# Eight of twenty modulation chunks moved from the first mixer into the first projection

## The reference

```python
for i in range(DEPTH):                                    # DEPTH = 2
    mod_x = jnp.split(jax.nn.silu(c) @ w_mod[i] + b_mod[i], 6, axis=-1)
    mod_c = jnp.split(jax.nn.silu(c_ctx) @ w_mod[i] + b_mod[i], 6, axis=-1)
    hx = modulate(rms_norm(x, norm1[i]), mod_x[0], mod_x[1])
    hc = modulate(rms_norm(ctx, norm1[i]), mod_c[0], mod_c[1])
    ...
# even mixer: proj = h @ w_in; qkv = silu(dwconv_centred(qkv, w)); q, k l2-normalised;
# gated DeltaNet over the chunks, both directions; gate, norm, @ w_out
```

## Time and profile before

| | before |
|---|---|
| three runs, us | 2581.56, 2587.11, 2586.36 |
| median, us | 2586.36 |
| the profiled execution, us | 2585.57 |
| its span, us | 2583.7 |
| mean granted clock of PE, share of full | 0.837 |
| PE / DVE / ACT / POOL busy, share of the span | 69% / 64% / 37% / 38% |
| DMA, mean over the span | 362 GB/s |

### The profile page before, as it was taken

How to read it: one execution, slowest core, us unless ns; L and a number is a source line. 1 busy time by engine, 2 the same in 40 slices (tenths; PEclk the granted TensorE clock), 3 DMA queues, 4 the chain that set the end, 5 groups by cost and what they waited for, 6 DMA issues and landing times.

```text
span 2583.7 us, 35131 instructions
## 1 busy us (share of the span) xinstructions
PE 1779.7 (69%) x13040; PEld 842.2 (33%) x13040; DVE 1664.7 (64%) x3921; ACT 956.5 (37%) x2624; POOL 979.3 (38%) x895
## 2 busy tenths in 40 slices
PE   5998889797867695557655565557957765565554
PEld 4877666445532251112211121113533311111111
DVE  2545657769996665677766776654466666766665
ACT  2411147444342332335533353333333433333333
POOL 2013123344443333444444444441023444445442
PEclk8999989898997897768887787778988877767777
DMA  8279769999899999999999999995168999999997
GB/s 310 98 252 324 279 254 370 390 387 393 335 366 417 415 398 409 421 397 419 419 419 421 394 421 419 421 421 212 66 266 356 421 421 421 392 412 421 421 421 292
DMA packets 181899, 936.20 MB, mean 362 GB/s; under 512 B 18128, under 2 KB 35408, under 8 KB 82400
## 3 DMA queue, kind: packets, MB, share of 16 engines
q0 software_dynamic: 114912, 808.16, 76.3%
q1 hardware_dynamic: 66816, 125.79, 13.4%
HBM read 932.74 MB, written 1.15 MB: 361 GB/s over the span
## 4 chain that ended last, share of the span: by engine, by line
DMA 40%; PE 32%; DVE 10%; issue 6%; ACT 6%; POOL 4%; another core or an unknown queue 0%; SPq 0%; DVEq 0%; POOLq 0%; ACTq 0%
DMA arena<-in_experts,expert_cur 38%; PE ps L1170 12%; PE ps L1950 11%; DVE arena L2031 5%; POOL arena L1863 4%; ACT diag L1883 2%; PE ps L1182 2%; DMA wring<-in_ev_w_in 2%; PE ps L1717 2%; PE ps L1195 2%; ACT coef L1879 1%; PE ps L1395 1%; DMA arena<-in_w_mod 1%; ACT acts L1878 1%; PE ps L1218 1%
## 5 line engine op out<-in xcount | busy, mean ns | idle before, releaser
L1950 PE MATMUL ps<-arena,diag 64*64 64x512 f32 x6144 | 1007.8, 784 | 664.9 <-ACT diag L1883 635.0
L1863 POOL DMA_INDIRECT arena<-in_experts,expert_cur x768 | 910.8, 1186 | 1333.8 <-PE ps L1950 1013.9
L2031 DVE CUSTOM_DVE_ANT_0 arena<-arena 128x1024 f32<-128x1024 f32 x768 | 943.3, 1229 | 613.9 <-DMA arena<-in_experts,expert_cur 605.6
L1950 PEld LDWEIGHTS ps<-arena,diag 64*64 64x64 f32 x6144 | 244.9, 161 | 1340.6 <-ACT diag L1883 961.7
L1878 ACT ACTIVATE acts<-dots 128x2 f32<-128x2 f32 x384 | 78.2, 204 | 1068.2 <-DVE dots L2031 1067.7
L1883 ACT ACTIVATE diag<-consts,coef 128x128 f32<-128x128 f32 x768 | 266.1, 393 | 12.5
L1879 ACT ACTIVATE coef<-acts,gate_cur 128x1 f32<-128x1 f32 x768 | 184.8, 288 | 12.6
L1170 PE MATMUL ps<-wring 128*128 128x256 f32 (+2 forms) x568 | 148.9, 414 | 29.6 <-DVE arena L815 15.3
L1170 PEld LDWEIGHTS ps<-wring 128*128 128x128 f32 x568 | 100.7, 195 | 94.7 <-issue 72.6
L1170 PE MATMUL ps<-arena,wring 128*128 128x256 f32 (+1 forms) x576 | 114.3, 357 | 6.4 <-issue 5.6
L1737 POOL DMA_DIRECT2D mods<-straight x48 | 26.7, 559 | 212.6 <-DVEq L1732 212.6
(11 more groups left out here) (331 smaller groups left out, 1813.0 us busy)
## 6 DMA issues: line engine op xcount, KB each, us to landing
wring<-in_w_mod SPq DMA_DIRECT2D x18, 2048.0 KB, 9.7
wring<-in_ev_w_in SPq DMA_DIRECT2D x14, 1024.0 KB, 24.6
arena<-in_w_mod SPq DMA_DIRECT2D x6, 2048.0 KB, 10.3
wring<-in_ev_w_in SPq DMA_DIRECT2D x6, 2048.0 KB, 10.4
arena<-in_experts,expert_cur POOLq DMA_INDIRECT x768, 11.8
wring<-in_p_w_q SPq DMA_DIRECT2D x5, 2048.0 KB, 27.4
wring<-in_ev_w_out SPq DMA_DIRECT2D x3, 2048.0 KB, 24.9
wring<-in_od_w_out SPq DMA_DIRECT2D x2, 2048.0 KB, 7.6
```

The costliest lines, as they stand in the source:

```text
L1863: nc.gpsimd.indirect_dma_start(ring[:, k % RING, :], None, table, bass.IndirectOffsetOnAxis(ap=expert_cur[:, par, k:k + 1], axis=0),).then ...
L1950: last = nc.tensor.matmul(ps[rows_of(o), sum_bank(i, c), :], diag[rows_of(i), slot, rows_of(i)], ring[rows_of(i), slot, D + 512 * c:D + 51 ...
L2031: ins = nc.vector.tensor_tensor_reduce(out=ring[:, slot, 0:D], in0=ring[:, slot, 0:D], in1=place, scale=1.0, scalar=0.0, op0=ALU.mult, op1 ...
```

## The change

Mod 4 to mod 11 leave the mixer and are multiplied between the stages of the first projection. The mixer keeps mod 12 to mod 23, still one a stage from stage 8 on, so now in stages 8 to 19. The list of first loads is written out by hand with its slots: the loads of the seven projection blocks and of the eight chunks alternate, and the chunks use slots 2 and 3 only. The sixteen loads behind them get hand-written slots too. The bodies of `mod_pe`, `mod_dve` and all sums are the same.

```diff
 def beside(main, rest, part=lambda n: None):
-    n = N_COLUMNS
+    n = N_COLUMNS + len(MODS_EARLY)
...
+def with_mods(main, part):
+
+
+    for i, _ in enumerate(main):
+        if i in MODS_EARLY:
+            part(N_COLUMNS + MODS_EARLY.index(i))
...
+MODS_EARLY = (2, 4, 5, 6, 8, 9, 10, 12)
 W_IN_ORDER = (3, 4, 5, 1, 2, 0, 6)
+FIRST_LOADS = [(3, 0), (4, 1), ("mod", 2), ("mod", 3), ("mod", 2), (5, 0), ("mod", 3), ("mod", 2), (1, 1), ("mod", 3),
+               ("mod", 2), (2, 0), ("mod", 3), (0, 2), (6, 3)]
...
-    loads = [(n, last, i % 4) for i, (n, last) in enumerate(loads)]
...
+    others = mods[n:]
+    others += [(("w_out0", 0, c), ("out0", 1, c)) for c in range(2)]
+    others += [(("w_q0", 0, c), ("q0", 0, 4 * c + 3)) for c in range(2)]
+    loads += [(name, last, (1, 0, 2, 3, 1, 3, 0, 2, 3, 1, 0, 2, 3, 0, 1, 2)[i]) for i, (name, last) in enumerate(others)]
...
-                whole(qkv_dve(dve, 0))
+                with_mods(qkv_dve(dve, 0), lambda n: mod_dve(dve, n))
...
-                whole(qkv_pe(pe, 0))
+                with_mods(qkv_pe(pe, 0), lambda n: mod_pe(pe, n))
```

More of the change, by code:

```diff
@@ L295, in weight_loads @@
     mods = [(("mod", i, c), ("mod", i, c)) for i, c in MODS]
-    loads = mods[:N_COLUMNS] + w_in_loads() + mods[N_COLUMNS:]
-    loads += [(("w_out0", 0, c), ("out0", 1, c)) for c in range(2)]
-    loads += [(("w_q0", 0, c), ("q0", 0, 4 * c + 3)) for c in range(2)]
-    loads = [(n, last, i % 4) for i, (n, last) in enumerate(loads)]
+    last_of, n = dict(w_in_loads()), N_COLUMNS
+    loads = [(*mod, i) for i, mod in enumerate(mods[:N_COLUMNS])]
+    for what, slot in FIRST_LOADS:
+        if what == "mod":
+            loads.append((*mods[n], slot))
+            n += 1
+        else:
+            loads.append((("w_in", what), last_of["w_in", what], slot))
+    assert n == N_COLUMNS + len(MODS_EARLY)
+    others = mods[n:]
+    others += [(("w_out0", 0, c), ("out0", 1, c)) for c in range(2)]
+    others += [(("w_q0", 0, c), ("q0", 0, 4 * c + 3)) for c in range(2)]
+    loads += [(name, last, (1, 0, 2, 3, 1, 3, 0, 2, 3, 1, 0, 2, 3, 0, 1, 2)[i]) for i, (name, last) in enumerate(others)]
     loads += [(("w_out0", 1, c), ("out0", 3, c), c) for c in range(2)]
@@ L1765, in _ @@
                 sp.dma_start(x[:, 2:4, :], T["x"].rearrange("(t p) d -> p t d", p=P)).then_inc(x_landed, 16)
-                for c in W_IN_ORDER:
-                    load_weight(sp, ("w_in", c), ktiles(T["ev_w_in"], c * 512, (c + 1) * 512))
-                for n in range(N_COLUMNS, len(MODS)):
+                n = N_COLUMNS
+                for what, _ in FIRST_LOADS:
+                    if what == "mod":
+                        load_mod(n)
+                        n += 1
+                    else:
+                        load_weight(sp, ("w_in", what), ktiles(T["ev_w_in"], what * 512, (what + 1) * 512))
+                for n in range(N_COLUMNS + len(MODS_EARLY), len(MODS)):
                     load_mod(n)
```

## The result

| | before | after |
|---|---|---|
| median of the runs, us | 2586.74 (2581.56 to 2593.54, 4 runs) | 2617.2 (2613.69 to 2621.85, 4 runs) |
| ratio, 95% interval | | 1.0122, 1.0096 to 1.0148 |
| the profiled execution, us | 2585.57 | 2621.85 |
| its span, us | 2583.7 | 2620.1 |
| granted clock of PE, share of full | 0.837 | 0.837 |

A forecast was written before the change was run, and what follows sets the result against it. PE was taken to bound the projection and mixer, with delay ahead of the gathering passing one for one to the end; 47.8 us late less 17.5 back is +30.3, 2617 us against the median, range 2603 to 2629.

The forecast's parts named there:

- end of pq5 later: Projection: 13.0 us of moved chunks, waits of 1.3 and 7.7, and 1.1 of clock make pq5 end 23.1 us later.
- from pq5's end to D: End of the projection: mod 11's load, matmuls and additions, two pairs of taps and over_length: 32.9 us instead of 9.7.
- the mixer starts late: Start of the mixer: 23.1 us at pq5's end, 23.2 more to D and 1.5 of clock, 47.8 us late.
- Waits for weights: Projection: loads queued on SP behind blocks waiting for a step make PE wait 1.3, 7.7 and 13.1 us.
- DVE behind mod 11: DVE's list holds mod 11 ahead of two taps and over_length pairs, 6.0 us each; PE idles about 9 us.
- The clock: Half-rate PE behind the three long waits: 1.1 us for mod 9, 1.1 for mod 11, 1.5 for D.
- Back in the mixer: Mixer: stages 8 to 19 stay at 72.1 us, stages 20 to 27 give back 17.5 us, 20.2 at most.
- Case B: Rival: pauses in stages 8 to 19 lift too, 35 us come back, +13 left, 2599 us; chance 0.10.
- Case C: Rival: pauses move with the instructions into the projection, four costing 5.6 us, 2622 to 2632 us; chance 0.10.
- D: As a case: loads bound the mixer, -20 us, 2566 us, if waits at mod 9 and 11 total under 4; chance 0.04.
- E: Rival: no change, the delay is taken up by unseen slack in front of the gathering; chance 0.04.
- that rule's sum: Mixer: pauses have a cause the change leaves alone, only 14.9 - 1.5 us come back, +34 us in sum.

The follow-up runs named there:

- e1: The change with the loads of mod 7, 9 and 11 put ahead of the projection blocks that wait for a step; DVE's list unchanged: 2599.5 us.
- e2: The change with only DVE's list edited, mod 11 standing ahead of taps(5) instead of taps(4): 2612.0 us.
- e8: The change with only mod 11's load swapped ahead of the projection block that waits for pq5: 2602.0 us.
- e6: The change with each chunk load from mod 4 on cut to one of eight row blocks, values not the reference's: 2592.9 us.
- e10: e3 with its twelve later chunks spread over stages 8 to 27 of the mixer: 2582.9 us, ratio to before 0.9986.
- e4: The kernel before with each load of mod 4 to 23 cut to one of eight row blocks, same instructions, values not the reference's: 2569.8 us.
- e3: The change with e1's load order and DVE taking each early chunk behind the taps and division of its step: 2587.5 us.
- e5: The change with loads and DVE as in e3, but seven early chunks: mod 10 behind pq5, mod 11 back in the mixer: 2586.4 us.
- e9: e5 with its thirteen later chunks spread over stages 8 to 27 of the mixer: 2581.2 us, ratio to before 0.9966.

## Why the prediction was right

Step by step, as the prediction put them, with times from the trace of after:

| step | predicted us | measured us |
|---|---|---|
| waits for mod 7, mod 9, mod 11 | 1.3, 7.7, 13.1 | 1.6, 7.1, 12.4 |
| end of pq5 later | 23.1 | 26.9 |
| from pq5's end to D | 32.9 | 33.3 |
| wait ahead of D | about 9 | 8.8 |
| the mixer starts late (measured at its first chunk) | 47.8 | 52.9 |
| stages 8 to 19 | 72.1 | 73.1 |
| stages 20 to 27 give back | 17.5 | 19.8 |
| sum | +30.3 | +34.0 at the mixer's end |

- **Waits for weights and DVE behind mod 11: right**, and shown apart from each other by e1, e2 and e8. Every row of DVE's list came as counted: 18.5 us of idle time, 1.6 from the chunk's end to the taps (counted as 1.4), 6.2 and 6.0 for the two pairs of taps and division (6.0 each), 2.5 to D (2.5).
- **The clock: a term that was too small, from a row misread.** I took 2.92 us for a chunk at half rate; behind the waits it took 3.59, and the product behind mod 9 0.3 us more. The chunk of 2.92 us began at 192.17 us, and the windows of before (PE busy and so on as above, then the clock) show its first part still at full clock:

```profile
192.00:193.00 1.00, 1.00 (x39) 0.90 (x39) 0.72 (x2) 0.00 (x0) 0.55 (x1) 0.96 1.04 399
193.00:194.00 1.00, 1.00 (x26) 0.78 (x21) 1.00 (x2) 0.00 (x0) 0.00 (x0) 0.50 1.05 406
```

D took 3.78 us instead of 2.05. The first step pq0 also ran at half rate for longer, 9.81 us against 8.6 before (the 15.60 us of two steps less the second's 7.0), with a start 0.6 us later (the clock rose to 1.00 at 53 us before, at 56 in after). These are most of the 3.8 us at pq5's end; the remainder are the projection's steps between the chunks, 0.1 to 0.4 us longer each than before.
- **Back in the mixer: nearly right as a sum, 18.7 for 17.5.** In stages 20 to 27 the pause of 1.2 us that I let stay didn't come, and the clock gave back more: PE is busy 17.4 us less there, 2.5 above the chunks' 14.9. The hand-overs cost 1.4 us, as taken. Over both stretches: 14.9 of chunks, 1.7 of clock, 3.7 of pauses, less 1.6 of new waits, is 18.7. What I did not see is that pauses and DVE's hand-overs lie over each other (e6, e10): a pause taken away is given back in part by a wait that it had hidden. That the pauses themselves are instructions that arrive late was read rightly; the last section shows it.
- **Case B** (the pauses lift in stages 8 to 19 too) fell: 13.0 us of them stay there, DMA share 0.86. **Case C** (pauses move into the projection) fell: PE's waits in after from 43 to 157 us, below, have no "issue" at all. **D** fell by its own condition, 19.5 us of waits at mod 9 and 11 against 4. **E** fell by the first gather.

```profile
PE ps L1737 <- DMA arena<-in_w_mod: 21.2, 3, 12.4
PE ps L1202 <- DVE arena L991: 8.8, 1, 8.8
PE ps L1190 <- ACT arena L816: 3.3, 1, 3.3
```

- **The number itself** is closer than its steps. The profiled executions differ by 36.3 us, 6.0 more than the sum of 30.3. They lie 4.7 us above (after) and 1.2 us below (before) the medians of their kernels, which makes up for 5.8 of that. So the 0.2 us between forecast and median is luck; the steps are good to some 6 us. The interval of the ratio, 25 to 38 us, doesn't tell the two sums apart. One sum of the forecast is off by a little: the upper end of the range, 2629 us, is 2628 by its own terms (47.8 - 12 + 5.6).
- **"Instruction fetch mechanics"** (the Trainium skill, "Runtime: NRT & Kernel Launch") calls the crossing between blocks of 256 instructions mostly hidden. With small loads the trace agrees: no pause at all in e4, 1.2 us in e6. With the DMA engines full the trace disagrees, by 16.7 us in the records and 17.4 in the medians. By that rule's sum, +34 us, the pauses would have stayed. That sum is what the trace shows at the mixer's end, but by other amounts: pq5's end was 3.8 us later than I had it, and 18.7 us came back, not 13.4.

## What to carry to other kernels

When work with a transfer of its own is moved forward, write down for its transfer what stands ahead of it on the issuing queue and when that is released, and do the same on every engine that takes up its results: here one chunk of eight made 23 of 30 us by standing last on both. Time that an engine is busy without its DMA engines is room only until the moved transfers fill it; count the bytes into the stretch (from 72 to 112 us the DMA share of 0.31 became 0.84 in the change and 1.00 in e1) before the gain is counted. And where small pauses and hand-over waits share a stretch, don't add their removals: the next one comes to light.

## What the hardware did that was not expected

**PE's instructions come by DMA, and late beside the weight loads.** PE's pauses, up to 2.8 us each, vanished when the weight loads were cut to an eighth (e4). The page of before has a DMA queue for instructions:

```profile
q8 instruction: 103, 1.69, 0.3%
```

PE's 13040 matmuls and 13040 weight loads are 26080 instructions. At the distance of the earlier trace rows, 256, that is 102 blocks, and the queue has 103 packets; I read it as PE's. From 182 to 185.4 us, up to the end of the pause at 185.40, the DMA queues of before show (packets, MB, share of 16 engines):

```profile
q1 hardware_dynamic: 639, 1.28, 101.4%
...
q8 instruction: 1, 0.02, 2.0%
```

One such packet, while the 16 engines are full with loads. It starts at 182.80 us and ends at 183.89, and PE goes on at 185.40. So it is with every pause: each of the 12 of the earlier trace rows ends 1.2 to 1.6 us after a packet of this queue has landed, and so do the 8 in the mixer of after, the 9 of e3 and the 9 of e5, the 4 of e9, the 2 of e10 and the 3 left in e6. PE's pauses end with the arrival of a block of instructions. The packet's own transfer is not longer for it: 1.0 to 1.3 us in the mixer of before, 0.9 to 1.7 in e4, where nothing pauses. So the delay lies ahead of its transfer. That it waits its turn among the weight loads is my reading, which e4 bears out; when the block was asked for is not in the trace.

**A load's latency under a full queue.** Alone a 2 MB load took 7.7 us; the second of two 13.7, in after 12.8 to 13.0; one issued behind others that were still under way 14.3 (e1, mod 10), 16.1 (after, mod 10) and 18.9 (after, the projection block issued at 124.74 us).

**Half rate isn't set by the wait's length alone.** Behind 4.4 us (e1) a chunk took 3.60 us against 1.93, as long as behind 12.4 us in after; behind 1.6 us it took 1.93. In between, 16 matmuls of a projection step took 5.41 us behind a wait of 2.74 us in e5, and 3.72, their full rate, behind one of 2.69 us in e9. The pauses in the mixer of before say the same: behind those of 1.89 us (end 191.79) and 2.80 us (end 246.67) the granted clock fell to 0.50, behind those of 1.92, 1.94, 2.19 and 2.20 us it stayed at 1.00. What makes the difference stays open.
